# The mixer's input projection, computed by Strassen's scheme over pairs of row chunks, in two passes of 900 columns

## What is computed

```python
def rmsnorm(x, g):
    xf = x.astype(F32)
    r = lax.rsqrt(jnp.mean(xf * xf, axis=-1, keepdims=True) + EPS)
    return (xf * r * g.astype(F32)).astype(x.dtype)
...
        xn = rmsnorm(x, p['g_mix'][l])
        proj = xn @ p['w_in'][l]
```

## Time and profile before

| | us |
|---|---|
| median of 3 runs | 2862.28 |
| lowest and highest | 2859.83, 2863.77 |
| the profiled execution | 2858.3 |
| its span | 2856.5 |
| mean granted TensorE clock, share of full | 0.991 |
| TensorE busy in the span | 2764.0 (97%) |
| VectorE, ScalarE, GpSimd busy | 1747.3, 1323.3, 431.2 |
| last eight projection matmuls start | 347.25 |

### The profile page before, as it was taken

One profiled execution on the slowest core, in us unless ns is written; L12 is line 12 of the kernel. 1 busy time (PEld: TensorE's weight loads), 2 busy tenths in 40 slices (PEclk: granted clock), 3 DMA queues, 4 the chain that ended last, 5 costly groups with the idle time before them and its releaser, 6 DMA issues. The chain is left out here.

```text
span 2856.5 us, 47085 instructions
## 1 busy us (share of the span) xinstructions
PE 2764.0 (97%) x17306; PEld 2646.6 (93%) x17306; DVE 1747.3 (61%) x2752; ACT 1323.3 (46%) x2520; POOL 431.2 (15%) x663
## 2 busy tenths in 40 slices
PE   8999999999999999999989999999999999999997
PEld 8888799989998989999989999999999998999997
DVE  5212167676767668877887777856544456445554
ACT  4212235454555445555655444773443366333442
POOL 2111021211112222222200000020000003001112
PEclk9999999999999999999999999999999999999998
DMA  5534266556655458777676666767665566755654
GB/s 186 195 128 144 89 206 189 187 161 217 215 165 162 134 201 254 258 265 259 219 281 208 211 212 221 252 204 250 203 200 172 188 204 198 244 185 188 205 194 120
DMA packets 373684, 569.44 MB, mean 199 GB/s; under 512 B 50578, under 2 KB 197586, under 8 KB 373458
## 3 DMA queue, kind: packets, MB, share of 16 engines
q1 hardware_dynamic: 371346, 566.31, 60.3%
q10 hardware_dynamic: 2112, 0.13, 0.0%
HBM read 415.33 MB, written 152.02 MB: 199 GB/s over the span
## 5 line engine op out<-in xcount | busy, mean ns | idle before, releaser
L2376 PE MATMUL f_ps<-f_xt,f_wh 128*128 128x348 f32 (+1 forms) x3696 | 670.6, 324 | 18.8 <-DVE both_high L2805 12.0
L2376 PEld LDWEIGHTS f_ps<-f_xt,f_wh 128*128 128x128 f32 x3696 | 604.9, 190 | 25.0 <-DVE both_high L2805 16.7
L2719 DVE TENSOR_TENSOR f_wl<-both_high,f_wh 128x512 fp32r<-128x512 f32 (+1 forms) x494 | 357.1, 736 | 203.8 <-ACT f_wh L2469 200.1
L2469 ACT ACTIVATE f_wh<-both_high 128x512 fp32r<-128x512 f32 (+1 forms) x494 | 298.8, 621 | 339.6 <-PE f_ps L2381 265.2
L2376 PE MATMUL f_ps<-f_gbuf,f_wh 128*128 128x348 f32 (+1 forms) x2112 | 383.6, 322 | 14.3 <-ACT f_ps L2582 6.3
L2381 PE MATMUL f_ps<-f_xt,f_wl 128*128 128x348 f32 (+1 forms) x1848 | 371.0, 323 | 0.0
L2376 PEld LDWEIGHTS f_ps<-f_gbuf,f_wh 128*128 128x128 f32 x2112 | 342.5, 188 | 19.9 <-ACT both_low L2587 10.0
L2381 PEld LDWEIGHTS f_ps<-f_xt,f_wl 128*128 128x128 f32 x1848 | 309.3, 189 | 0.0
L829 PE MATMUL pp<-gxh,gwh 128*128 128x416 f32 x792 | 290.9, 367 | 1.5 <-DVE gxl L778 1.3
L829 PE MATMUL pp<-gxh,gwl 128*128 128x416 f32 x792 | 279.4, 353 | 0.0
L829 PE MATMUL pp<-gxl,gwh 128*128 128x416 f32 x792 | 278.1, 351 | 0.0
(11 more groups left out here) (342 smaller groups left out, 4441.8 us busy)
## 6 DMA issues: line engine op xcount, KB each, us to landing
both_high<-in_w_up SPq DMA_DIRECT2D x220, 256.0 KB, 4.2
f_wh<-up_parts SPq DMA_DIRECT2D x176, 256.0 KB, 2.7
f_wl<-up_parts SPq DMA_DIRECT2D x176, 256.0 KB, 3.0
both_low<-in_w_gate SPq DMA_DIRECT2D x80, 512.0 KB, 4.6
up_parts<-f_wh SPq DMA_DIRECT2D x88, 256.0 KB, 2.9
up_parts<-f_wl SPq DMA_DIRECT2D x88, 256.0 KB, 3.4
both_high<-in_w_br SPq DMA_DIRECT2D x40, 512.0 KB, 4.7
both_high<-in_w_out SPq DMA_DIRECT2D x40, 512.0 KB, 4.5
```

The lines of the kernel that those rows point to most:

```text
L2376: pe.matmul(out, cut(wh, k), x(k), start=(start and k == 0 and x is xhi), stop=False, skip_group_check=not start or not stop)
L2469: act.activation(ring_slot(wh, e, w), src, ACT.Copy).then_inc(ev("w_hi"), 1)
L2719: dve.tensor_tensor(ring_slot(wl, e, w), src, ring_slot(wh, e, w).bitcast(F32), ALU.subtract).then_inc(ev("w_lo"), 1)
```

## The change

The 16 chunks are taken as eight pairs, and the 1800 columns as two passes over 900 (`STEPS_A` = 16 steps of one pair in one pass). In a step, the pair is a 2 by 2 block matrix a11 .. a22 (first index: chunk of the pair, second: which half of the 1024 features), the 900 columns of weights are the blocks b11 .. b22 (first index: half of the features, second: which 450 columns). The first two steps (`CLASSIC`) form the four results with eight block products (`EIGHT`); the other fourteen use seven products (`STRASSEN`) of sums of blocks: s1 = a21+a22, s2 = s1+a11, s3 = a21+a11, s4 = s2+a12 of x, and t1 = b11-b12, t3 = b12-b22, t2 = t3-b11, t4 = b21+t2 of the weights. A block product is 12 matmuls of 450 columns (4 feature slices, three matmuls each).

The x sums are made on VectorE, five a step, and each of the seven operands is split anew, 512 elements wide, on ScalarE (high) and VectorE (low). The weight sums are made once a pass, t1 on GpSimd and t3, t2, t4 on VectorE, each 1800 elements wide, and each of the seven weight operands of a pass is split 1800 wide. The second pass has the same seven buffers: its splits stand in step 7, each behind the last product that reads the buffer. Between the products ScalarE copies partial results from one PSUM bank to another so that the next product adds on top (`first_seed`, `next_seeds`), and keeps one in SBUF (`keep_value`); VectorE forms the results c22 and c21. The seventh product waits for c22, since it adds into the bank that c22 is read from. Each result of 128 by 450 goes to memory by itself. Normalisation is done by pair: two squares and two sums over slices, one group of two one-column matmuls, one broadcast of 256 columns. For later pairs the group `sums` stands behind the first product of a step and `rows` behind the second, one block product apart. The second pass reads x again, already normalised, from `xn_rows`. The small group is multiplied in two parts instead of four. Positions (s, j) in the tables mean behind product j of step s.

```diff
-GROUP_A = 3
+PAIRS_A = CHUNKS // 2
+HALF = WROW // 4
+KH = KT // 2
+CLASSIC = 2
+STEPS_A = 2 * PAIRS_A
...
-SAMPLE = GROUP_A
-CHUNK_AT = [*range(GROUP_A), CHUNKS, *range(GROUP_A, CHUNKS)]
-PIECES = [(c, s0 + c - c0, 264 if c == 1536 else 256) for c0, s0, w in ROWS for c in range(c0, c0 + w - 8, 256)]
...
+STRASSEN = [("a11", "b11", 0), ("s3", "t3", 2), ("s2", "t2", 1), ("a12", "b21", 0), ("s1", "t1", 3), ("a22", "t4", 4), ("s4", "b22", 3)]
+EIGHT = [("a11", "b11", 0), ("a21", "b11", 1), ("a12", "b21", 0), ("a22", "b21", 1),
+         ("a11", "b12", 2), ("a21", "b12", 3), ("a12", "b22", 2), ("a22", "b22", 3)]
+X_HOME = {"a11": 0, "a12": 1, "a22": 2, "a21": 3, "s1": 3, "s2": 4, "s3": 5, "s4": 6}
+W_HOME = {"b11": 0, "b21": 1, "b22": 2, "t1": 3, "t2": 4, "t3": 5, "t4": 6, "b12": 6}
...
+def products_of(s):
+    return [(x, w, m if m != 2 or s == 0 else 4) for x, w, m in EIGHT] if s < CLASSIC else STRASSEN
...
+W_OPS = [(0, t) for t in ("b11", "b21", "b12", "b22", "t3", "t1", "t2", "t4")] + [(1, x[1]) for x in STRASSEN]
...
+REDUCES = after([((1, 0), (0, 3)), ((1, 1), (0, 4)), (("s", 0), (0, 7)), ((2, 0), (1, 1)), ((2, 1), (1, 2))]
...
+SUMS = after([(1, (0, 5)), (2, (1, 0)), (3, (1, 3))] + [(p + 1, (p - 1, 0)) for p in LATER])
...
+W_SPLITS = after([((0, "t3"), (0, 7)), ((0, "t1"), (1, 0)), ((0, "t2"), (1, 2)), ((0, "t4"), (1, 6))]
+                 + [((1, x[1]), (PAIRS_A - 1 + (j + 1) // 7, (j + 1) % 7)) for j, x in enumerate(STRASSEN)])
+T3_SUMS = {(0, 5): 0, (6, 3): 1}
...
+    wh = [sb(f"a_wh{i}", [P, KH, HALF], F32R) for i in range(7)]
+    wl = [sb(f"a_wl{i}", [P, KH, HALF], F32R) for i in range(7)]
+    xh = [sb(f"a_xh{i}", [P, KH, P], F32R) for i in range(7)]
+    xl = [sb(f"a_xl{i}", [P, KH, P], F32R) for i in range(7)]
...
-    first = [(n, j) for j in range(G) for n in range(G - 1)] + [(G - 1, j) for j in range(G)] + [(n, j) for j in range(G, NP) for n in range(G)]
-    order = [(n, PIECES[j][0], PIECES[j][2], j + 1) for n, j in first] + [(n, c, w, NP) for n in range(G + 1, N) for c, _, w in ROWS]
...
+        def weights(h, t):
+            if h:
+                sp.wait_ge(ev("w_lo"), 8)
+                sp.wait_ge(ev("samp_proj"), 1)
...
+        def sums(h):
+            wait(pe, "ssum_ready", SQ_END[h])
+            wait(pe, "rvar_ready", h)
+            for i in range(1 if NORMS[h] == "s" else 2):
+                mm = pe.matmul(pst[:, i:i + 1], ssum[:, i, :], ones[:, 0:1], start=True, stop=True)
+            mm.then_inc(ev("st_done"), 1)
...
+        def bank_ready(s, j):
+
+            n = s - CLASSIC
+            if n < 0:
+                if j in (0, 1, 4, 5):
+                    wait(pe, {0: "c11", 1: "c21", 4: "c12", 5: "c22"}[j], s)
+            elif j == 0:
+                wait(pe, "c11", s)
+            elif j == 1:
+                wait(pe, "value", n)
+                if n == 0:
+                    wait(pe, "c12", s)
+            elif j == 2:
+                wait(pe, "b_seeded", n + 1)
+            elif j == 4:
+                wait(pe, "d_seeded", n + 1)
+            elif j == 5:
+                wait(pe, "e_seeded", n + 1)
+            elif j == 6:
+                wait(pe, "c22", s + 1)
...
+        def product(s, j):
+            at, bt, m = products_of(s)[j]
+            fresh = j in ((0, 1, 4, 5) if s < CLASSIC else (0, 1))
+            bank_ready(s, j)
+            nx, nw = X_AT[entry_of(s), at] + 1, W_AT[pass_of(s), bt] + 1
+            x, w = X_HOME[at], W_HOME[bt]
+            o = ps[m][:, 0:HALF]
+            wait(pe, "w_hi", nw)
+            wait(pe, "x_hi", nx)
+            for k in range(KH):
+                pe.matmul(o, xh[x][:, k, :], wh[w][:, k, :], start=(fresh and k == 0), stop=False, skip_group_check=not fresh)
+            wait(pe, "x_lo", nx)
+            for k in range(KH):
+                pe.matmul(o, xl[x][:, k, :], wh[w][:, k, :], start=False, stop=False, skip_group_check=not fresh)
+            wait(pe, "w_lo", nw)
+            for k in range(KH):
+                mm = pe.matmul(o, xh[x][:, k, :], wl[w][:, k, :], start=False, stop=(k == KH - 1), skip_group_check=not fresh)
+            mm.then_inc(ev("proj"), 1)
...
+        def first_seed(s):
+            n = s - CLASSIC
+            done(s, 0)
+            wait(act, "d_seeded", n)
+            wait(act, "e_seeded", n)
+            if n == 0:
+                wait(act, "c21", s)
+            act.activation(ps[1][:, 0:HALF], ps[0][:, 0:HALF], ACT.Copy).then_inc(ev("b_seeded"), 1)
+
+        def keep_value(s):
+            done(s, 1)
+            wait(act, "c22", s)
+            wait(act, "c21", s)
+            wait(act, "out_c21", 16 * s)
+            act.activation(value, ps[2][:, 0:HALF], ACT.Copy).then_inc(ev("value"), 1)
+
+        def next_seeds(s):
+            done(s, 2)
+            wait(act, "c12", s)
+            wait(act, "c22", s)
+            act.activation(ps[3][:, 0:HALF], ps[1][:, 0:HALF], ACT.Copy).then_inc(ev("d_seeded"), 1)
+            wait(act, "c21", s)
+            act.activation(ps[4][:, 0:HALF], ps[1][:, 0:HALF], ACT.Copy, scale=-1.0).then_inc(ev("e_seeded"), 1)
...
+        def t3_sum(h):
+            weights_in(dve, "b12", h)
+            weights_in(dve, "b22", h)
+            wait(dve, "w_lo", W_AT[h - 1, "t4"] + 1 if h else 0)
+            dve.tensor_tensor(t_sum, raw["b12"], raw["b22"], ALU.subtract).then_inc(ev("t3_ready"), 1)
+
+        def w_low(h, t):
+            wait(dve, "w_hi", W_AT[h, t] + 1)
+            have_weights(dve, h, t)
+            wait(dve, "proj", w_before(h, t))
+            dve.tensor_tensor(wl[W_HOME[t]][:], weight_block(t), wh[W_HOME[t]][:].bitcast(F32), ALU.subtract).then_inc(ev("w_lo"), 1)
+            if t == "t3":
+                wait(dve, "w_lo", W_AT[h, t] + 1)
+                weights_in(dve, "b11", h)
+                dve.tensor_tensor(t_sum, t_sum, raw["b11"], ALU.subtract).then_inc(ev("t2_ready"), 1)
+            elif t == "t2":
+                wait(dve, "w_lo", W_AT[h, t] + 1)
...
+        for s in range(STEPS_A):
+            for j in range(len(products_of(s))):
+                if s >= CLASSIC and j == 4:
+                    dve.wait_ge(ev("proj"), FIRST_A[s] + j + 1)
+                    dve.wait_ge(ev("value"), s - CLASSIC + 1)
+                    wait(dve, "out_c22", 16 * s)
+                    dve.tensor_tensor(out["c22"], value, ps[3][:, 0:HALF], ALU.subtract).then_inc(ev("c22"), 1)
+                elif s >= CLASSIC and j == 5:
+                    dve.wait_ge(ev("proj"), FIRST_A[s] + j + 1)
+                    wait(dve, "c22", s + 1)
+                    dve.tensor_tensor(value, ps[4][:, 0:HALF], value, ALU.add).then_inc(ev("c21"), 1)
+                for h in VARIANCES.get((s, j), ()):
+                    variance(h)
+                for h in NORMED.get((s, j), ()):
+                    normed(h)
+                for e, t in X_SPLITS.get((s, j), ()):
+                    x_low(e, t)
+                if (s, j) in T3_SUMS:
+                    t3_sum(T3_SUMS[s, j])
+                for h, t in W_SPLITS.get((s, j), ()):
+                    w_low(h, t)
+                for g, i in REDUCES.get((s, j), ()):
+                    reduce(g, i)
...
-        sp.wait_ge(ev("last_rows"), 16)
+        sp.wait_ge(ev("last_rows"), 64)
```

597 lines of the change are left out of this document (332 added, 265 removed).

## The result

The changed kernel takes 2882.16 us (median of 4 runs, 2881.25 to 2884.78) against 2861.06 us for the kernel before (median of 4, 2858.77 to 2863.77): a ratio of 1.0075, 95% interval 1.0057 to 1.0092. It is 21 us slower, where the prediction had 2863 and a range of 2848 to 2880. The direction that I held least likely came true, and the range ended 2 us short.

What follows compares the result with a forecast made beforehand. TensorE's matmuls were taken to bound the stage: 310.3 us without waits, plus waits 29.2, clock 9.3 and end 0.15, gives 349.0 against 348.4 (+0.6), so a median of 2862.9 us, range 2848 to 2880.

Steps and rivals of the forecast that it cites:

- The direction that I held least likely: Whole kernel: slower, over 2868.0 us, was given 0.26, against faster 0.31 and same 0.43.
- The products: TensorE, whole stage: 450-wide matmuls cost 206 ns each, a block product 2.47 us, all of them 281.6 us.
- The small group: TensorE: 225 columns cost 3.2 us, twice 3.2 against 6.7 before.
- The long waits: TensorE waits 6.0 and 6.2 us for `sums` in step 1, and 6.6 us before step 7's last product.
- the loop: Steps 3 to 6, broadcast to next `sums`: 18.4 us round against 18.0 for TensorE, some 0.4 to 1.0 lost a step.
- a sign of being wrong: Steps 3 to 6 above 20 us would show the prediction wrong.
- Rival (b): Steps 3 to 6: x lands late, about 3 us a step, 12 in all, giving 2875 us; chance 0.23.
- The clock: TensorE's clock falls to 0.50 behind waits of 6.0, 6.2 and 6.6 us, costing 3.1 each, 9.3 in all.
- That of 2.7 none: Step 2: the 2.7 us wait costs no clock, as nothing followed 2.81 us idle in the earlier trace.
- The start: Before step 0: first product at 16.1 us, its first 3.4 us at half speed, 1.7 lost.
- Pass 2: Steps 8 to 15: 17.3 us each, waits set at nothing; above 17.6 a step would be wrong.
- The 38 us that the stage without waits would gain are given back: Whole stage: 310.3 us without waits, but waits and clock bring it to 349.0 against 348.4 before.

Runs made afterwards that it cites:

- later splits: Changed kernel with five of seven second-pass weight splits one product later; stage ends at 359.6 us against 372.1, steps 7 and 8 take 35.7 instead of 43.2.
- the new order: Changed kernel with sums over slices first, weights spread, splits later, and steps 0 to 2, 7, 8 reordered; 2837.13 us, ratio 0.9925 to the kernel before.
- waits up and down: Two kernels: the new order plus five waits by hand in steps 10 to 14, lengthening in one, shortening in the other; stage ends 344.8 and 347.3 us.
- one part undone: The new order with the second pass's four weight blocks all sent in step 3 again, ahead of output rows; stage ends at 329.5 us instead of 322.9.
- the first kernel: The new order plus hand-made waits behind product 3 of steps 10 to 14, lengthening from 1 to 6 pieces of useless work; stage ends at 344.8 us.

## Why the prediction was wrong, point by point

**The products** were right: 206 ns per matmul, 2.47 us per product. The small group too (steps 9 and 10 differ by 20.62 - 17.26 = 3.4 us, 3.2 taken). The count of matmuls before was off, 1752 and not 1536, since the first three chunks go in seven pieces; at the prediction's own price per column that changes its sum by 0.2 us.

**The long waits** of steps 1 and 7 were right in place, releaser and size: 6.12 and 7.25 for 6.0 and 6.2, 5.95 for 6.6. The 1.05 more in the second is the hold, with 0.5 the other way: t4's sum took 3.61 us instead of 2.03, beside GpSimd's product, and without that product the wait was 5.68. The experiment with the later splits shows that the chain in step 7 was the cause, as the prediction laid it.

**The step that failed** is the loop, "18.4 us round against 18.0 for TensorE, some 0.4 to 1.0 a step". Steps 4 to 6 took 22.7 to 24.9 us, above the 20 that the prediction itself had named as a sign of being wrong. I had used the hold between VectorE and GpSimd in one direction only, for GpSimd's power behind a VectorE operation, and never for the gain's product, which runs in front of every sum over slices: 1.66 us on a chain that I myself called without slack. Cutting the product short (15.4 us) and changing the order (12.6 us) each took that away, except in step 4, where the copy into `value` waited for a transfer, for which the prediction had no term. In step 2 the same hold made 5.49 us of the 2.7 predicted (2.19 without it).

**Rival (b)** came near in size by luck and was wrong in its place. It said 2875 by x landing late, and 2882 came. But with the order changed and the weights spread the loop ran in 18.13 us with x loaded as before. The transfer that was late was an output: c21's rows, behind the weights that the rival had named, and only in step 4 (7 us of it once the other wait was gone). The prediction asked what the weights do to the loads of x, and not what they do to the output rows behind them on SyncE, and who waits for those.

**The clock** was mis-sized. I gave 9.3 us for three falls and nothing for waits under 3 us. There were eight falls, at a price of 16.6 us by the estimate above: four with waits of 5.5 us and more, and four with waits of 1.7 to 2.8, of which a second execution had three, and that with the later splits, whose waits are the same up to step 6, none. "That of 2.7 none" rested on a single row.

**The start** came 2.2 us later: GpSimd's power took 2.45 us behind b11's low split, so that the broadcast ran at 15.0, the first normalising ended at 17.5, and ScalarE's split of it at 18.2.

**Pass 2** at 17.3 a step was right but for step 11, 18.7, with waits of 0.67 and 0.32, and for step 8, 17.65. With the next phase's loads spread over four steps, in the new order, step 11 took 17.27; that edit was not tested alone.

In terms of the sum: waits 37.2 instead of 29.2 (+8.0), the clock 16.6 instead of 9.3 (+7.3), the start +2.2, and 5.6 that the sum had no term for, of which 0.25 us of handing over at each of thirteen waits would be 3.2. The other 2.4 are open.

**"The 38 us that the stage without waits would gain are given back"** was right as a mechanism, and more than it was given back. The new order got 25.5 of them, by the end of the stage in one execution.

## What to carry to other kernels

When matmuls are taken away, write down for each wait of TensorE the queue ahead of its releaser, with every operation at the length that it has beside its neighbours: a product on GpSimd lengthens the next two-input operation on VectorE until it is done. Put what TensorE waits for (small sums for a norm, a result that frees a bank) ahead of wide work with slack in the same place; here that alone was worth 12.6 of the lost 23.7 us, and the order as a whole turned 21 us slower into 23 us faster. A transfer that frees a buffer belongs ahead of bulk loads on its queue, and when one wait is removed, look for the next one that it covered.

## What the runs showed of the hardware

- **The hold goes both ways.** GpSimd's power of 0.55 us takes 2.45 behind a VectorE operation of 2.03 (11.67 in the start), and VectorE's split of 0.69 takes 2.35 behind a GpSimd product of 1.90 us; with that product at 0.24 it takes 0.71. The Trainium skill, "Perfetto Trace Analysis", section "Optimizing Scalar/DVE Operations", says that the two share an SBUF read port which a VectorE operation that uses both ports holds as an exclusive lock. The trace agrees, and shows that the one that came first keeps it, GpSimd too: VectorE operations with two SBUF inputs that met a running GpSimd product ended 0.55 to 0.60 us (512 elements) or 1.9 us (1800) behind its end. VectorE's sum over slices, with one input, ran beside GpSimd's product in 1.9 to 2.0 us.
- **The clock's falls behind short waits differ from execution to execution of one kernel,** with waits equal to 0.03 us: loss 3.4, 1.7 or none behind 2.8 us, 1.7 or none behind 1.75. In the kernel with the new order, the same two waits of 0.90 and 1.18 us, close together in step 0, went with a loss of 1.7, none, 3.4 and 1.7 in four executions (its own, those with waits up and down, and that with one part undone), and step 0 took 27.0, 24.7, 27.7 and 27.6 us. I expect a few us of scatter in any kernel with such waits.
- **Half clock costs only while TensorE works:** 0.45 us for each us worked at a granted clock of 0.50, in six falls from 2.9 to 5.9 us of work. That is why the fall in step 14 of the first kernel, of which TensorE stood through 3.1 us, cost 1.7 us, and those with waits of 3.9 us, with 1.2 and 1.5 us of standing, 2.6 and 2.4.
